# Attention on one Trainium2 core: the second head's sample score tile is issued behind the first head's value products

## What is computed

```python
s = jnp.einsum('bqhd,bkhd->bhqk', q, k, preferred_element_type=jnp.float32) * (q.shape[-1] ** -0.5)
if c_q is not None:
    s = s + (c_q[:, :, :, None] - c_k[:, :, None, :])
s = jnp.where(mask[None, None], s, -jnp.inf)
p = jax.nn.softmax(s, axis=-1).astype(v.dtype)
return jnp.einsum('bhqk,bkhd->bqhd', p, v)
```

## Time and profile before

| | |
|---|---|
| median of three runs | 2466.8 us |
| profiled execution | 2467.75 us |
| its span in the trace | 2465.9 us |
| PE busy | 2274.8 us, 92% of the span |
| DVE busy | 1715.8 us, 70% |
| ACT busy | 1075.7 us, 44% |
| POOL busy | 324.1 us, 13% |

### The profile page before, as it was taken

One profiled execution on the slowest core, in us unless ns is written; L12 is line 12 of the kernel. 1 busy time (PEld: TensorE's weight loads), 2 busy tenths in 40 slices (PEclk: granted clock), 3 DMA queues, 4 the chain that ended last, 5 costly groups with the idle time before them and its releaser, 6 DMA issues. The chain is left out here.

```text
span 2465.9 us, 45118 instructions
## 1 busy us (share of the span) xinstructions
PE 2274.8 (92%) x16514; PEld 2183.8 (89%) x16514; DVE 1715.8 (70%) x2706; ACT 1075.7 (44%) x1799; POOL 324.1 (13%) x284
## 2 busy tenths in 40 slices
PE   4999999688988999999999999999978888999997
PEld 4999999677877999999987999999867778999997
DVE  8976974457666698498445995895366648975973
ACT  5532542355555454154323552453246545532541
POOL 1000001134333100000113000001143311000001
PEclk9999999788889999999999999999978889999998
DMA  2222232000000222222223222222121112222221
GB/s 106 102 88 92 102 103 73 24 19 19 9 10 27 79 101 98 81 103 102 73 68 115 104 107 89 87 107 83 66 52 45 45 35 77 102 98 82 102 105 60
DMA packets 72810, 187.55 MB, mean 76 GB/s; under 512 B 40720, under 2 KB 42288, under 8 KB 61440
## 3 DMA queue, kind: packets, MB, share of 16 engines
q1 hardware_dynamic: 71424, 181.67, 21.6%
q0 software_dynamic: 1280, 4.49, 0.5%
HBM read 178.79 MB, written 7.35 MB: 75 GB/s over the span
## 5 line engine op out<-in xcount | busy, mean ns | idle before, releaser
L565 PE MATMUL ps<-xs_hi,w_hi 128*128 128x272 f32 x1408 | 410.3, 291 | 49.8 <-DVE w_lo_more L1538 28.3
L567 PE MATMUL ps<-xs_hi,w_lo 128*128 128x272 f32 x1408 | 408.0, 290 | 0.0
L566 PE MATMUL ps<-xs_lo,w_hi 128*128 128x272 f32 x1408 | 407.2, 289 | 0.0
L1043 ACT ACTIVATE w_hi<-raw 128x1408 fp32r<-128x1408 f32 (+3 forms) x124 | 146.0, 1183 | 506.4 <-PE ps L590 246.0
L1072 ACT ACTIVATE w_hi<-w_blocks 128x1024 fp32r<-128x1024 f32 x176 | 186.8, 1061 | 323.1 <-PE ps L567 159.1
L565 PEld LDWEIGHTS ps<-xs_hi,w_hi 128*128 128x128 f32 x1408 | 266.5, 189 | 53.6 <-issue 29.7
L565 PE MATMUL ps<-xs_hi,w_hi_more 128*128 128x272 f32 x1056 | 306.5, 290 | 2.4 <-ACT scratch L1118 1.8
L566 PE MATMUL ps<-xs_lo,w_hi_more 128*128 128x272 f32 x1056 | 305.9, 290 | 0.0
L590 PE MATMUL ps<-hid_hi,w_hi 128*128 128x272 f32 x1312 | 273.3, 290 | 9.1 <-DVE w_lo L1508 5.5
L590 PE MATMUL ps<-hid_lo,w_hi 128*128 128x272 f32 x1312 | 271.8, 289 | 0.0
L590 PE MATMUL ps<-hid_hi,w_lo 128*128 128x272 f32 x1312 | 271.8, 288 | 0.0
(11 more groups left out here) (257 smaller groups left out, 5165.2 us busy)
## 6 DMA issues: line engine op xcount, KB each, us to landing
w_blocks<-w_ffn_in SPq DMA_DIRECT2D x88, 1024.0 KB, 4.8
raw<-w_ffn_out SPq DMA_DIRECT2D x64, 704.0 KB, 4.1
raw<-w_b_kv SPq DMA_DIRECT2D x16, 512.0 KB, 3.3
raw<-w_a_out SPq DMA_DIRECT2D x8, 512.0 KB, 3.2
raw<-w_b_q SPq DMA_DIRECT2D x8, 512.0 KB, 3.3
raw<-w_b_out SPq DMA_DIRECT2D x8, 512.0 KB, 3.3
raw<-w_a_in SPq DMA_DIRECT2D x4, 672.0 KB, 4.0
raw<-w_a_qup SPq DMA_DIRECT2D x8, 288.0 KB, 2.7
```

The lines of the kernel that those rows point to most:

```text
L565: pe.matmul(out, lhs[0], rhs[0], start=start, stop=False, skip_group_check=more)
L566: pe.matmul(out, lhs[0], rhs[1], start=False, stop=False, skip_group_check=more)
L567: return pe.matmul(out, lhs[1], rhs[0], start=False, stop=stop, skip_group_check=more)
L1043: act.activation(wh[par][:, 0:n], raw[par][:, 0:n], ACT.Copy).then_inc(w_hi, 1)
```

## The change

The second head's sample score tile s14 is taken out of `first_head` and issued right behind pv0 inside the staging. In MLA the order becomes s13, tq0, tq1, pv0, s14, tp0; in FoX s13, tq0, tq1, tp0, pv0, s14, tp1. Its followers move too. ACT's `exp14` goes from the end of `first_head` to behind the eviction of q1; DVE's m14 goes between the lows of q0 and q1, r14 and d14 behind the low of q1 (in MLA behind kn). s14 reads the second head's queries in `qT`, which the eviction of q1 overwrites, so ACT gets a new wait: q1's eviction waits for s14. In the last pair s14, m14, exp14, r14 and d14 follow pv0 directly. `values` gets a list of tiles, always all four. No instruction on data is added or removed.

```diff
 ATT = {
-    "pe": sum([[f"t0{j}", f"s1{j}"] for j in range(4)], []) + ["s14", "pv0"] + ...
+    "pe": sum([[f"t0{j}", f"s1{j}"] for j in range(4)], []) + ["pv0", "s14"] + ...
...
-    "dve": [..., "ps0", "pt03", "r12", "m14", "r13", "r14", "d14"]
+    "dve": [..., "ps0", "pt03", "r12", "r13", "m14", "r14", "d14"]
...
                 def first_head(p, stages):
                     for j in range(4):
                         turn(0, j, p, uses, before)
                         scores(1, j, p)
+
+                def first_values(p):
+                    values(0, p)
                     scores(1, 4, p)
...
-                        turn_staged(p + 1, uses, before, lambda: values(0, p))
+                        turn_staged(p + 1, uses, before, lambda: first_values(p))
...
 # ACT
-                def stage(it):
+                def stage(it, last=None):
...
                             act.wait_ge(*stg["pe"].at(f"{name}{hh}", it))
+                            if (name, hh) == ("tq", 1) and last is not None:
+                                act.wait_ge(*att["pe"].at("s14", last))
...
+                        if name == "tq" and last is not None:
+                            exp(1, 4, last)
...
-                    for u in range(2, 5):
+                    for u in range(2, 4):
                         exp(1, u, p)
...
 # DVE
                             low(out[1][0:D, c], ps[0:D, banks[f"{name}{hh}"], :], out[0][0:D, c],
                                 None if g is None else g[0:D, :], inc)
+                            if (name, hh) == ("tq", 0) and last is not None:
+                                top(1, 4, last)
                         if mla and step == "q":
                             norm_keys(it)
+                        if step == "q" and last is not None:
+                            inverse_sum(1, 4, last)
...
-                    top(1, 4, p)
                     inverse_sum(1, 3, p)
-                    inverse_sum(1, 4, p)
```

## The result

The changed kernel takes 2509.86 us (median of 4 runs, 2508.99 to 2511.88) against 2466.38 us, the median of four runs of the kernel before: 1.0177 times as long, 95% interval 1.0165 to 1.019. The forecast was 2483, with a range up to 2500. The direction was right, the size was not: +43.5 us against +16. The profiled execution took 2511.88 us (span 2510.1), 44.1 more than the one of before.

A forecast was written before the change was run, and what follows sets the result against it. TensorE, 92% busy, was taken as the bound, its clock low in both attention stages, with a gap ahead of s14. MLA +6.5 and FoX +9.6 made +16.1 on 2467.75; less 0.95 for the median, 2483 us, range 2458 to 2500.

The forecast's parts named there:

- The gap: TensorE's idle between s13 and s14, 1.7 us, would become gaps of about 0.35 and 0.55.
- FoX's t10: FoX pairs 1 to 6: t10 at 9.7 us after s13 against 8.80 at full clock, waiting for c0's low.
- MLA's tp0: MLA pairs 1 to 6: tp0 at 7.7 us after s13 against 9.14, with 3.0 us of idle ahead.
- FoX pair 0: First FoX pair: s14 and its followers stand behind pv0's wait for POOL's staged values, t10 later by 2.4 us.
- the last pairs: Last pair, without staging: s14 swaps with pv0 and t13 comes several us later, priced at 0.
- FoX's clock term: FoX pairs 1 to 6: clock fall in the dense stretch from t10, +2.8 a pair, the middle of 1.6 and 4.0.
- tp0's step: MLA pairs 1 to 6: tp0 at 7.7 us after s13 against 9.14, so 1.45 earlier a pair.
- The clock term behind tp0: MLA pairs 1 to 6: one half-clock spell a pair in key transposes and projections, +2.2 us each.
- The full-cost rival: Every FoX pair like the 17.31 one (+2.4), MLA slow already at pv0 (+3): +37, 2504 us; chance 0.11.
- the rule: TensorE idling briefly but often swings between clock levels, so low-clock spells stay wherever the idle is moved; speaks against the change.

The follow-up runs named there:

- e3: Changed kernel plus filler products that compute nothing, where TensorE idles in the staging of both stages, other order unchanged: 2466.84 us.
- e9: Kernel before plus filler products in both stages, ahead of s14 and FoX's t10 and ahead of MLA tp0's wait for the keys: 2449.88 us.
- e5: Changed kernel, but in the last pair of each stage s14, m14 and exp14 stand where they stood before: 2498.51 us.
- e4: Kernel before plus 9 filler products ahead of s14 in both stages and 4 ahead of FoX's t10: 2458.58 us.
- e7: Kernel before with tq0 and tq1 ahead of s14 in both stages, s14 still ahead of pv0, last pair unchanged: 2469.79 us.
- e8: Kernel before plus filler products in FoX alone, 9 ahead of s14 and 4 ahead of t10: 2451.55 us.
- e10: Kernel before with tq0 and tq1 ahead of s14 in FoX alone, s14 still ahead of pv0: 2459.53 us.

## Why the prediction was wrong in size

**What held.** The gap went as said, to 0.58 and 0.46 (0.35 and 0.55 forecast). pv0 ran at full clock in FoX. FoX's t10 came at 9.93 (9.7 forecast), MLA's tp0 at 8.3 at nearly full clock (7.7) in three of the six pairs 1 to 6, with 2.9 us of idle ahead (3.0). FoX pair 0 lost 2.8 up to t10 (2.4; the working starts at 1833.3, and from the 1833.55 of the earlier trace rows it gives 2.6). The direction and the mechanism, idle moved to where a fall of the clock hits dense work, are shown by e3 beside e9: 26.5 us of the loss go when both orders are filled.

**The steps that failed.** Of the 28 us that the forecast lacked on the profiled execution, FoX's six pairs hold 8.3, FoX's pair 0 5.3, the last pairs 8.4, MLA's pairs 4.1, and some 2 lie outside.

**FoX's clock term.** With the last pairs this is the largest error. Of the two prices in the earlier trace rows, 1.6 and 4.0, I took the middle, "as part of a fall may be over by t10". It never was. Every dense stretch took 17.3 to 18.0, the dearer row or more. The row nearest to the new state was the pair whose clock fell right after t10, and that was the one to take: 9.7 + 0.2 + 17.3 = 27.2 against 24.8 is +14.4 in six pairs; measured +15.5, forecast +7.2.

**FoX pair 0.** I counted the wait up to t10 (+2.4) and not what follows. The clock had been low from 1826 on and stayed so to 1873.86, through a dense stretch of 18.34 against 13.48. The missing term is +4.9.

**The last pairs.** "s14 swaps with pv0, 0" was wrong, twice, 8.4 us in all. I looked for who waits for d14, and not at what is queued behind exp14 on ACT: pt10's eviction. I also overlooked that pv0 waits for POOL's values, which come after the time that PE is free. e5 shows it: -11 with the old order there.

**MLA.** tp0's step was 0.6 too early, because pv0 has to wait for POOL's values (0.73 us of idle ahead of it) where I counted only pt03. In two of six pairs pv0 ran at the lower clock as well, which makes it 10.4 and 10.6, and in a third partly so, 9.1. So over pairs 1 to 6 the forecast gain of 1.45 a pair was nothing: 9.16 against 9.19. The clock term behind tp0 was 2.2 forecast, 1.4 measured on average over pairs 0 to 5: two of the six stretches of before already carried the price, and I charged it in full on top of a mean that had it. Where the fall hit behind tp0 alone it was dearer than that row, 32.1 against 29.0 in three pairs. Net +10.6 over pairs 0 to 6 against +6.5.

**The rivals.** The full-cost rival (2504) came nearest, with my lowest chance, 0.11. That a spell once started stays in this kind of work is what FoX shows (+15.5 in six pairs, its term was +14.4); why it stays was not tested. That its sum came near is in part luck: its MLA term was too large (+18 for six pairs, with +6.8 measured in pairs 1 to 6), and this made up for much of the last pairs and of FoX's pair 0, which it lacks as well. The range was too narrow by the two terms that I had set to 0, and these had no bound in it.

**On the rule.** In the changed kernel a gap of 2.87 us ahead of tp0 and three gaps of 0.6 to 1.1 in FoX were followed by falls, and e3 beside e9 prices what they add at 26.5 us. The Trainium skill, page "TensorE: Matmul & The Clock Gate", section "A second HAM failure mode: psum-queue depth-cycling", says that idling in small portions makes the clock swing; the trace agrees, and so do e4 and e7 in MLA. By the section "HAM oscillation — how this bites in real kernels" of the same page, which warns only of longer single gaps, the new ones would have cost nothing; here the trace differs. FoX's pair 0 is an exception that the prediction overlooked when it cited that section: PE stands 6.60 us ahead of pv0 there, and stood 4.94 before.

## What to carry to other kernels

Before idle time of the tensor engine is moved, ask what stands behind its new place: a half-clock spell hidden under another engine's chain costs little (here 1.0 us for 6.8), in dense matmul work it costs a third of its length or more (2.2 us for 6.9 in MLA, 4.0 for about 10 in FoX), and it may last long into that work. Where the clock falls in the trace, price the new order with the row whose spell lies where the new one will, not with a mean. And where a step moves, read the queue behind each of its followers, in the last iteration too.

## What was not expected of the hardware

A busy engine alone did not bring the clock back. Three stretches of the changed kernel, one after the other: the thin one, the low spell, and what came next.

```profile
1914.80:1918.22 3.42, 2.40 (x19) 1.94 (x20) 2.66 (x8) 1.94 (x6) 0.00 (x0) 1.00 0.25 56
...
1918.22:1928.46 10.24, 10.24 (x43) 9.37 (x41) 5.06 (x15) 3.95 (x13) 4.04 (x7) 0.50 0.15 34
...
1928.46:1931.88 3.42, 3.42 (x29) 3.28 (x28) 1.44 (x4) 1.69 (x5) 0.00 (x0) 1.00 0.00 0
```

PE was busy for all of the 10.24 us at half clock, with transposes and 66-row score products, then with pv1, and the clock rose only during pv1's last products, those of the sample queries. What the clock answers to was not tried further and stays open. And products that compute nothing, 13 a pair in FoX (e8), took 14.9 us off the kernel before, where the best reordering tried here (e10) took 6.9.
